# Retention variance reduced to 128x4 and spread by transposes, rotary projections scaled at eviction, and compression one tile later, in a two-layer hybrid mixer

## What is computed

```
h = rms_norm(x, norm1_g);  z = h @ w_in
y_a = b * causal_conv3(c * h3)                      # short convolution
y_b = nsa(...)       # 8 heads of 64: compressed, selected, window attention
y_c = retention(z_q, z_k, z_v, z_g)                 # 4 heads of 128
y_d = pool_mixer(u)
merged = sum_n (y_n @ w_branch[n]) * sigmoid(gate_n)
x = x + merged @ w_o
x = x + (silu(conv3(h2 @ w_up_gate)) * (h2 @ w_up_val)) @ w_down
```

```
o = (o - mean(o)) * rsqrt(var(o) + EPS) * gn_g * silu(z_g)
```

## Time and profile before

| | before |
|---|---|
| median of 3 runs | 2092.7 us |
| profiled execution | 2092.94 us |
| its span | 2091.2 us |
| TensorE busy | 2044.3 us (98%) |
| VectorE busy | 1216.9 us (58%) |
| GpSimd busy | 917.6 us (44%) |
| ScalarE busy | 682.9 us (33%) |
| mean granted TensorE clock | 0.992 |

### The profile page before, as it was taken

One profiled execution on the slowest core, in us unless ns is written; L12 is line 12 of the kernel. 1 busy time (PEld: TensorE's weight loads), 2 busy tenths in 40 slices (PEclk: granted clock), 3 DMA queues, 4 the chain that ended last, 5 costly groups with the idle time before them and its releaser, 6 DMA issues.

```text
span 2091.2 us, 31895 instructions
## 1 busy us (share of the span) xinstructions
PE 2044.3 (98%) x9764; PEld 1637.6 (78%) x9764; DVE 1216.9 (58%) x1811; ACT 682.9 (33%) x1001; POOL 917.6 (44%) x672
## 2 busy tenths in 40 slices
PE   8999999999999999999999999899999999999997
PEld 6777667888888888888877777678888888888886
DVE  7766866523226888862257677663322278888522
ACT  5255523333232322222233554232323232222222
POOL 3422223444444555545544212335444455555552
PEclk9999999999999999999999999999999999999998
DMA  5311122223222222223233112222222222232333
GB/s 208 96 62 52 62 74 93 81 100 100 93 98 99 93 97 93 100 85 119 91 120 101 51 52 65 88 86 91 98 97 96 100 91 92 99 100 92 102 107 104
DMA packets 57431, 194.88 MB, mean 93 GB/s; under 512 B 7040, under 2 KB 7552, under 8 KB 57216
## 3 DMA queue, kind: packets, MB, share of 16 engines
q1 hardware_dynamic: 52576, 186.17, 26.6%
q10 hardware_dynamic: 4768, 7.61, 1.4%
HBM read 186.67 MB, written 2.10 MB: 90 GB/s over the span
## 4 chain that ended last, share of the span: by engine, by line
PE 87%; DVE 8%; issue 3%; ACT 1%; ACTq 0%; DMA 0%; DVEq 0%; SPq 0%
PE acc L1185 27%; PE acc L1187 26%; PE acc L1186 26%; PE o L1385 2%; PE s L1359 2%; PE t L1367 1%; PE o L1418 1%; PE s L1408 1%; DVE pT L967 1%; DVE pT L964 1%; DVE win_k L775 0%; DVE rk L759 0%; PE s L1268 0%; DMA w_raw<-weights_dram 0%; DVE rstd L748 0%
## 5 line engine op out<-in xcount | busy, mean ns | idle before, releaser
L433 POOL TENSOR_TENSOR w_lo<-w_raw,w_hi 128x512 fp32r<-128x512 f32 x668 | 917.4, 1394 | 1148.5 <-ACT w_hi L455 1132.3
L1185 PE MATMUL acc<-xg_hi,w_hi 128*128 128x512 f32 x1904 | 771.2, 405 | 5.6 <-DVE xg_lo L697 3.0
L1187 PE MATMUL acc<-xg_hi,w_lo 128*128 128x512 f32 x1904 | 744.0, 391 | 0.0
L1186 PE MATMUL acc<-xg_lo,w_hi 128*128 128x512 f32 x1904 | 743.3, 390 | 0.0
L455 ACT ACTIVATE w_hi<-w_raw 128x1024 fp32r<-128x1024 f32 x336 | 355.3, 1057 | 822.9 <-PE acc L1187 777.7
L1185 PEld LDWEIGHTS acc<-xg_hi,w_hi 128*128 128x128 f32 x1904 | 358.4, 188 | 114.9 <-issue 29.0
L1186 PEld LDWEIGHTS acc<-xg_lo,w_hi 128*128 128x128 f32 x1904 | 358.8, 188 | 77.8 <-issue 7.3
L1187 PEld LDWEIGHTS acc<-xg_hi,w_lo 128*128 128x128 f32 x1904 | 358.4, 188 | 76.7
L1062 DVE TENSOR_TENSOR work<-acc,rstd 128x512 f32<-128x512 f32 x64 | 44.1, 689 | 256.2 <-PE acc L1187 256.2
L1186 PE MATMUL acc<-act_lo,w_hi 128*128 128x512 f32 x352 | 136.9, 389 | 0.0
L1185 PE MATMUL acc<-act_hi,w_hi 128*128 128x512 f32 x352 | 136.9, 389 | 0.0
(11 more groups left out here) (207 smaller groups left out, 2237.4 us busy)
## 6 DMA issues: line engine op xcount, KB each, us to landing
w_raw<-weights_dram SPq DMA_DIRECT2D x339, 512.0 KB, 3.3
x<-xT_dram SPq DMA_DIRECT2D x8, 256.0 KB, 6.4
rot<-rq ACTq DMA_DIRECT2D x16, 128.0 KB
rot<-rk ACTq DMA_DIRECT2D x16, 128.0 KB
dec<-decay_dram ACTq DMA_DIRECT2D x8, 256.0 KB, 3.2
out_dram<-x SPq DMA_DIRECT2D x8, 256.0 KB, 2.7
con<-consts_dram SPq DMA_DIRECT2D x1, 1406.0 KB, 11.1
w1k<-w_dram SPq DMA_DIRECT2D x2, 512.0 KB, 8.8
```

What stands on the lines that cost most here:

```text
L433: nc.gpsimd.tensor_tensor(w_lo[:, slot, part], w_raw[:, slot, part], w_hi[:, slot, part].bitcast(F32), ALU.subtract).then_inc(lo_ready, 1)
L1185: mm(tile, w_h, right_hi, start=first, stop=False)
L1186: mm(tile, w_h, right_lo, start=False, stop=False)
L1187: return mm(tile, w_l, right_hi, start=False, stop=last)
```

## The change

Seven things change.

- **Variance.** `ret_var` on TensorE is four matmuls with the squares as weights and one column of ones, which give variances as 128x4 (tokens on partitions). ScalarE's root and VectorE's reciprocal work on 128x4 (`ret_inv`). A new step `ret_spread` at n0+8 turns four broadcast columns back into 128x512 in an S bank, by transposes. `ret_end` reads this bank.
- **Rotation.** Once a layer VectorE makes `cos_rms` and `sin_rms` (rstd times cosine and sine), behind `kc`. The eviction of `rq` and `rk` multiplies by `cos_rms`. ScalarE copies the two halves crossed out of the same PSUM bank (`swap_halves`), and only then the bank is free. VectorE multiplies by `sin_rms` and adds. The DMAs go. The VectorE part moves to the end of the following tile.
- **Tangent.** `rg_t` is computed at n0+2 (`ret_tanh`), `ret_gate` on VectorE is at n0+4.
- **Places.** `ret_end`, `ret_hi` and `ret_split` move to n0+9, +10 and +11 (head 3: +9, +11, +13).
- **Compression** stands behind tile 6, its second layer behind tile 8; VectorE's steps are reordered to this.
- **Start.** 14 instead of 10 matmuls on the cleared tile.
- **End.** The four matmuls that spread the last root are transposes.

```diff
-    SIDE[_n0 + 5].append(("ret_gate", _h))
+    SIDE[_n0 + 2].append(("ret_tanh", _h))
+    SIDE[_n0 + 4].append(("ret_gate", _h))
     SIDE[_n0 + 6].append(("ret_var", _h))
     SIDE[_n0 + 7].append(("ret_inverse", _h))
+    SIDE[_n0 + 8].append(("ret_spread", _h))
...
-    SIDE[RET_SLOT[_h] + (11, 8, 8, 10)[_h]].append(("ret_end", _h))
-    SIDE[RET_SLOT[_h] + (12, 9, 9, 12)[_h]].append(("ret_hi", _h))
-    SIDE[RET_SLOT[_h] + (14, 10, 10, 14)[_h]].append(("ret_split", _h))
+    SIDE[RET_SLOT[_h] + (9, 9, 9, 9)[_h]].append(("ret_end", _h))
+    SIDE[RET_SLOT[_h] + (10, 10, 10, 11)[_h]].append(("ret_hi", _h))
+    SIDE[RET_SLOT[_h] + (11, 11, 11, 13)[_h]].append(("ret_split", _h))
...
-        if B_TILES[_b][0] in ("rq", "rk") and _k < 2:
-            SIDE[4 * (_b + 2) + (1 if B_TILES[_b][0] == "rq" else 0) + _k].insert(0, ("rotate", B_TILES[_b], _k))
+    if B_TILES[_b][0] in ("rq", "rk"):
+        SIDE[4 * (_b + 1) + 3].insert(0, ("rotate", B_TILES[_b]))
...
+            def swap_halves(L, tile):
+
+                T, i = A_GROUPS + B_TILES.index(tile), ROT[tile]
+                act.wait_ge(v_made, v_count(L, ("took", *tile)))
+                nc.scalar.activation(rot[0:64, i % 2, :], acc[T % 2][64:128, :], ACT.Copy)
+                nc.scalar.activation(rot[64:128, i % 2, :], acc[T % 2][0:64, :], ACT.Copy).then_inc(acc_free, 1)
...
                     if 0 < b and B_TILES[b - 1][0] in ("rq", "rk"):
-                        rotate_partners(L, B_TILES[b - 1])
+                        swap_halves(L, B_TILES[b - 1])
...
-                                nc.scalar.activation(pT[:, 1, :], s_of(e)[:, :], ACT.Sqrt, bias=C("eps", 1),
+                                nc.scalar.activation(ret_inv, s_of(e)[:, 0:QT], ACT.Sqrt, bias=C("eps", 1),
                                                      scale=1.0 / RD).then_inc(a_made, 1)
...
+                    dve.wait_ge(acc_free, 1 + L * TILES + (T + 2))
+                    then(ve.tensor_tensor(r, r, sin_rms[:, :], ALU.mult))
+                    v_end(ve.tensor_tensor(z, z, r, ALU.add), e[1])
...
                 v_end(ve.tensor_tensor(kc[:, 0:NCMP], kc[:, 0:NCMP], kc_rot[:, 0:NCMP], ALU.add), "kc")
+                ve.tensor_tensor(cos_rms[:, :], rstd[:, :], C("cos_r", S), ALU.mult).then_inc(chain, 1)
+                then.n += 1
+                then(ve.tensor_tensor(sin_rms[:, :], rstd[:, :], C("sin_r", S), ALU.mult))
...
-                    then(ve.reciprocal(pT[:, 1, 0:S // 2], pT[:, 1, 0:S // 2]))
-
                 def ret_inverse(e):
-                    s_end(ve.reciprocal(pT[:, 1, S // 2:S], pT[:, 1, S // 2:S]), ("ret_var", e[1]), wait=True)
+
+                    dve.wait_ge(a_made, a_count(L, ("ret_var", e[1])))
+                    s_end(ve.reciprocal(ret_inv, ret_inv), ("ret_var", e[1]))
...
+                        v_end(ve.tensor_tensor((rq if kind == "rq" else rk)[:, i % 2, :], acc[T % 2][:, :], cos_rms[:, :], ALU.mult),
+                              ("took", kind, i), wait=True)
...
-                    if g == 5:
+                    if g == 6:
                         compress()
-                    if g == 7:
+                    if g == 8:
                         pe.wait_ge(v_made, v_count(L, "hid"))
...
-                    mm(b[:, :], ones, pT[:, 1, :], start=True, stop=True).then_inc(s_done, 1)
+                    for t in range(QT):
+                        ins = mm(b[:, t:t + 1], pT[:, 1, t * P:(t + 1) * P], ones[:, 0:1], start=True, stop=True)
+                    ins.then_inc(s_done, 1)
+
+                def ret_spread(e):
+                    pe.wait_ge(s_free, 1 + s_use(L, ("ret_var", e[1])) + 1)
+                    b = s_begin(e)
+                    last_wait()
+                    for t in range(QT):
+                        ins = nc.tensor.transpose(b[:, t * P:(t + 1) * P], spread(ret_inv[:, t:t + 1], [[0, P]]), ident)
+                    ins.then_inc(s_done, 1)
...
-                ins = mm(s_bank[1][:, t * P:(t + 1) * P], spread(rstd[:, t:t + 1], [[0, P]]), ident, start=True, stop=True)
+                ins = nc.tensor.transpose(s_bank[1][:, t * P:(t + 1) * P], spread(rstd[:, t:t + 1], [[0, P]]), ident)
```

More of the change, by code:

```diff
@@ L139 @@
 S_USES = ["sumsq1", "hid_k", "hid_v", "kc", "vc", "kc_swap"]
-S_USES += [_e for _e in SEQUENCE if _e[0] in ("gate", "cmp_keys", "cmp_scores", "scores", "ret_scores", "ret_var", "pool")]
+S_USES += [_e for _e in SEQUENCE if _e[0] in ("gate", "cmp_keys", "cmp_scores", "scores", "ret_scores", "ret_var", "ret_spread", "pool")]
 S_USES += ["sumsq2"]
@@ L149 @@
 A_MADE = ["hid", "gate"]
-for _slot in SIDE:
+for _n, _slot in enumerate(SIDE):
     for _e in _slot:
-        if _e[0] in ("cmp_scores", "scores", "ret_gate", "ret_var", "ret_hi", "attn_hi") or _e[0] == "conv" and _e[2] == 2 or _e[0] == "ret_values" and _e[2] == QT - 1:
+        if _e[0] in ("cmp_scores", "scores", "ret_tanh", "ret_var", "ret_hi", "attn_hi") or _e[0] == "conv" and _e[2] == 2 or _e[0] == "ret_values" and _e[2] == QT - 1:
             A_MADE.append(_e)
@@ L159 @@
             V_MADE.append(("u", _e[1]))
-        if _e[0] == "rotate" and _e[2] == 1:
+        if _e[0] == "rotate":
             V_MADE.append(_e[1])
+    if _n % 4 == 3 and B_TILES[_n // 4][0] in ("rq", "rk"):
+        V_MADE.append(("took", *B_TILES[_n // 4]))
 V_MADE.append("branches")
@@ L830, in _ @@
                 rotate("q0", qT[:, 0, :], "cos_a", "sin_a")
+                take(8, qT[:, 2, :])
+                rotate("q1", qT[:, 1, :], "cos_a", "sin_a")
                 s_wait("kc")
@@ L1178, in _ @@
             pe.wait_ge(zero_made, 1)
-            for _ in range(10):
+            for _ in range(14):
                 mm(acc[1][:, 0:P], rstd[:, 0:P], rstd[:, 0:P], start=True, stop=True)
@@ L1437, in _ @@
                          "cmp_turn": cmp_turn, "ret_scores": ret_scores, "ret_values": ret_values,
-                         "ret_turn": ret_turn, "ret_var": ret_var, "pool": pool}
+                         "ret_turn": ret_turn, "ret_var": ret_var, "ret_spread": ret_spread, "pool": pool}
                 for b in range(B_GROUPS):
```

50 lines of the change are left out of this document (24 added, 26 removed).

## The result

The changed kernel takes 2075.98 us (median of 4 runs, 2074.31 to 2076.59); beside it the kernel before took 2093.11 us (4 runs, 2092.09 to 2094.68). The ratio is 0.9916, with a 95% interval of 0.9899 to 0.9933. The forecast was 2075 us. The profiled execution has a span of 2074.8 us, 16.4 us shorter than before, and a mean granted clock of 0.996 instead of 0.992. Of the four executions three took 2075.90 to 2076.59 us at a mean clock of 0.996, and one 2074.31 us at 0.998; the first, at 2076.59 us, is the one that was profiled.

The account below looks back on a forecast made before the run. TensorE was taken as the bound, busy 2044.3 of 2091.2 us, with VectorE binding for moments. Terms -13.2 - 4.8 + 4.2 - 6.8 + 3.4 - 1.0 = -18.2 us, from 2092.9 to 2075 us; range 2068 to 2086 us.

Parts of the forecast that it names:

- Waits in retention: TensorE's waits at heads 1 to 3 and for the rotated k go, head 0's stay: gain 13.2 us.
- Clock: Half-clock stretches around the end of head 1's wait, in both layers, go with that wait: gain 4.8 us.
- TensorE's own work: In retention, the new `ret_var` costs +0.6 us and `ret_spread` +3.6 us over eight heads: together +4.2 us.
- Compression: One tile later TensorE no longer waits for the windows, 0.4 us a layer added for banks: net -6.8 us.
- The seam: Two VectorE products between `kc` and the gates' eviction make TensorE wait 1.7 us a layer ahead of `cmp_keys`: +3.4 us.
- Start: Four more warm-up matmuls may keep the clock up, 0 to -1.3 us; taken as 0.
- end: The last spread, by transposes, has four records instead of eight: -1.0 us, all on the path.
- The wait at head 1: Rival: in retention this wait shrinks but stays, 2.5 of 3.9 us left, clock falls as before: 2084.5 us; chance 0.17.
- VectorE is the bound of the A stage: Rival: nothing of the 6.8 us gain is left and the new products are paid in full: 2083.7 us; chance 0.12.
- ScalarE holding the banks: Rival: q and k banks come back late after ScalarE's copies, 12 tiles wait 2 us each: 2098.7 us; chance 0.05.
- The small operations: Rival: one-column matmuls cost 1.5 us and a spread 1.0 us on TensorE: 2083.5 us; chance 0.08.

Follow-up runs that it names:

- e4: Changed kernel with two reciprocals of 128x256 (3.5 us) put back on VectorE behind each head's small reciprocal; 2074.67 us (one execution).
- e5: Changed kernel with four reciprocals of 128x256 (7 us) added on VectorE behind each head's small reciprocal; 2106.19 us.
- e2: Changed kernel with compression put back behind tile 5, its second layer behind tile 7, VectorE's steps there as before; 2078.9 us (one execution).
- e7: Kernel before with the rotation part alone, old reciprocals of 128x512 kept; 2101.67 us (4 runs), ratio to before 1.0044.
- e1: Changed kernel with the products cos_rms and sin_rms moved behind the copies of the compressed keys' scores; 2077.36 us (median of 4), ratio to before 0.9923.
- e3: Changed kernel with compression back behind tile 5 and the cos_rms and sin_rms products behind the copies of the compressed keys' scores; 2081.08 us (one execution).
- e10: e9 with the eviction of tile 5 moved ahead of the rotation of k 1; 2068.74 us (4 runs), ratio to before 0.9884.
- e9: Changed kernel with the cos_rms and sin_rms products moved up behind the argument of gelu, ahead of tile 7's eviction; 2070.88 us (4 runs), ratio to before 0.9895.
- e8: Changed kernel with 10 instead of 14 warm-up matmuls on the cleared tile at the start; 2076.05 us (one execution).
- e11: Changed kernel with the last spread made by matmuls of two passes again instead of transposes; 2075.42 us (one execution).
- e6: Kernel before with the variance part alone, rotation, compression, start and end old; 2079.05 us (4 runs), ratio to before 0.9933.

## Why the prediction was right, and where it was not

**Waits in retention (13.2 us): right.** They went, and head 0's stayed, 2.9 us in two layers. The margin that I had put at about 3 us is 3.5 us or a little more (e4), and less than 7 (e5).

**Clock (4.8 us): right.** Layer 1's retention shows it. Of the waits 3.86, 1.40, 0.51, 0.29 and 0.50 us went, 6.6 in all, and 1.7 us of clock; 0.48 us of new work in each of four heads is 1.9 us back. That makes 6.4 us. Measured without the disturbance of the seam (e2): 304.39 - 296.82 = 7.6 us. In layer 0 the same sum, with its 3.1 us of clock and waits of 6.6 us, gives 7.8 us, and 305.76 - 296.80 = 9.0 us were measured.

**What the sum left out: the price of taking up the stream again.** The missing 1.2 us of each layer are in the starts around a wait. In the kernel before, the first scores of head 1 without a wait and of head 2 with one:

```profile
1315.81 0.40 PE L1187 MATMUL acc<-xg_hi,w_lo 128*128 128x512 f32 x1
1316.05 1.02 PE L1408 MATMUL s<-rq,rk 128*128 128x512 f32 x2
1316.50 0.80 PE L1185 MATMUL acc<-xg_hi,w_hi 128*128 128x512 f32 x1
1317.13 0.40 PE L1186 MATMUL acc<-xg_lo,w_hi 128*128 128x512 f32 x1
```

```profile
1349.98 0.40 PE L1187 MATMUL acc<-xg_hi,w_lo 128*128 128x512 f32 x1
1351.78 1.10 PE L1408 MATMUL s<-rq,rk 128*128 128x512 f32 x2 [1.40 <-DVE rk L761]
1352.31 0.79 PE L1185 MATMUL acc<-xg_hi,w_hi 128*128 128x512 f32 x1
1352.94 0.40 PE L1186 MATMUL acc<-xg_lo,w_hi 128*128 128x512 f32 x1
```

From the product ahead to the second behind it is 1.32 us, and 2.96 - 1.40 = 1.56 us with the wait taken off. So this wait costs 0.24 us more than its row says. Waits at a plain product show the same: in e7 from the product ahead of the wait of 3.18 us to the second behind it is 3.87 us, 0.69 us without the wait, against 0.45 us in the stream. Five waits a layer make 1.2 us, 2.4 us in all that the sum of retention lacked, and this closes both layers' sums.

**TensorE's own work (+4.2 us): right (3.9 us).** `ret_var` and `ret_spread` at head 0 of the changed kernel, with the product ahead and the second behind each:

```profile
273.67 0.39 PE L1205 MATMUL acc<-xg_hi,w_lo 128*128 128x512 f32 x1
273.89 0.95 PE L1444 MATMUL s<-con,pT 128*128 128x1 f32 x8
...
275.03 0.40 PE L1204 MATMUL acc<-xg_lo,w_hi 128*128 128x512 f32 x1
...
277.34 0.39 PE L1205 MATMUL acc<-xg_hi,w_lo 128*128 128x512 f32 x1
277.57 0.60 PE L1452 MATMUL s<-con,small 128*128 128x128 f32 x4
...
278.24 0.39 PE L1204 MATMUL acc<-xg_lo,w_hi 128*128 128x512 f32 x1
```

The first is 1.36 us less two plain gaps of 0.23, 0.90 us, where I took 0.94 (before 0.87). The second is 0.90 - 0.45 = 0.45 us, as taken. The estimate of the prediction by the Trainium skill, "TensorE: Matmul & The Clock Gate", section "LDWEIGHTS (loading the stationary operand)", 0.85 us for the eight loads, is near the 0.90 us too; the trace agrees with its rule that the columns of the stationary operand set the price, and 128 times fewer moving columns bought nothing.

**Compression (-6.8 us): the step that failed.** It gave 4.2 us (2.1 a layer, e1 to e3). The direction was right, but I put the wait for the banks of tile 7 and of the transposes at 0.4 us a layer where they were 1.09 (layer 1: 0.84) + 0.33 us, with 0.24 us for each. In layer 0 that makes 3.49 + 0.24 + 0.3 (the transposes) - 1.09 - 0.33 - 0.48 = 2.1 us, where e1 to e3 measured 2.3 and 1.8. I had taken the eviction of tile 5 for where it was before; it hung on an operation that took 0.69 us before and 1.66 us beside GpSimd's longer work. e10 shows that 1 us a layer of this was a matter of order. The clock, at half for 3.4 us of each A stage of the kernel before (0.57 on average from 50 to 54 us), was no further gain: the 64 small matmuls of `compress` took 3.56 us from first to last start there, and 3.57 us at full clock in the changed kernel. "At half clock work takes twice as long", as the prediction has it, holds for the products and not for them.

**The seam (+3.4 us): right in place, and too small.** It costs 2.0 us a layer in the A stage by e1 to e3 (1.9 by e9) where I had 1.7: the wait itself is 1.8 us, and a wait costs more than its row. What I did not see is that the clock can fall behind it: in layer 1 of the changed kernel (and of e8) a stretch at half makes retention 1.6 us longer (298.40 against 296.8 in e2, e4, e9 and e10). Whether it falls differs from kernel to kernel and layer to layer, and, by the mean clocks and times of the changed kernel's four executions, from one execution to the next; what decides it stays open. The same luck is in every single execution told of here: 1.6 us can go either way without the kernel being different.

**Start (0) and end (-1.0 us): right.** The clock of the start was gained, and given back to the inputs. The last spread took 1.12 us, against 2.08 us (e11).

**The sum.** -18.2 us forecast, -16.4 measured. The A stages came out 3.1 us worse (-0.3 against -3.4), retention 1.1 us better (-14.9 against -13.8: 2.4 us of taking up the stream, less 1.6 us of clock, and 0.3 us of roundings), the rest 0.2 us better. Two errors of opposite sign made the total look better than its terms.

**The rivals.** The wait at head 1 did not stay. "VectorE is the bound of the A stage" described the outcome of that stage, no gain, but not its cause: the gain of compression is there (e2), the seam eats it, and e9 shows idle time on VectorE that a bound engine would not have. ScalarE holding the banks did not occur in the changed kernel, and does in e7, with waits of 3.1 to 3.2 us where I had put 2, and four of them instead of twelve. The small operations cost what they should.

## What to carry to other kernels

Read the neighbour's idle time before placing new work. The same 2.5 us of VectorE cost 5 us in all ahead of the gates' eviction, no less behind `cmp_keys` (e1), and nothing in a gap 27 us earlier (e9), which VectorE's own rows show. Try each part of a change alone and price them together: the variance alone gives 13.4 of the 17.1 us, the rotation alone loses 9.3 us, and the rotation and the tangent's place on top of the variance lose nothing. And a wait of the engine that bounds the kernel costs more than its row: 0.24 us here to take up the stream, and at times a stretch at half clock. Since that comes and goes between executions, a difference of 2 us needs more than one execution, or the rows of its stage.

## What the runs showed of the hardware

- A wait of TensorE between two products of this stream cost 0.24 us beyond its recorded idle time, at full clock, whether it was 1.4 us long (before) or 3.2 us (e7).
- The granted clock fell behind waits of 1.65 us (e1, both layers) and 1.8 us (the changed kernel, layer 1, not layer 0). It did not fall behind the 1.4 us at head 1 in e6, nor behind one of 3.19 us in e7 (at 1348.70 us), and in the kernel before the waits of 3.9 us cost 3.1 us in one layer and 1.7 in the other.
- A VectorE operation on 128x512 fp32 with both operands in SBUF took 0.68 to 0.69 us with GpSimd idle (136 of them in the changed kernel's trace), and up to 1.8 us beside it; all 106 of over 1 us in the changed kernel's trace had GpSimd busy during at least 65% of their time. With an operand in PSUM none of 342 was slowed. The same instruction changed from one to the other between kernels: `sin_rms` 1.76 us at the seam and 0.68 us in e9, the second product of `ret_end` 1.70 us and 0.69 us in e4.
- ScalarE's copy of 64x512 out of PSUM with crossed halves took 0.59 us, as long as one of 128x512.
- The 64 matmuls of `compress` (128x64 weights, 62 columns) took 3.56 us with most of them at half clock (before) and 3.57 us at full clock (after); products of 512 columns start 0.43 us apart at half and 0.23 us apart at full clock (e8).
